# Layer 1's modulation: one product with ones against transposes and a sum along the free axis

## The chip, the core and the metric

The kernel runs on one core of a Trainium2 chip. The metric is the device time of one execution in microseconds (us). Instructions run on five engines: TensorE (PE in the profile), VectorE (DVE), ScalarE (ACT), GpSimd (POOL) and SyncE (SP, which issues the weight transfers). Engines are tied together by semaphores that the kernel sets and waits for by hand.

## The reference, cut to what matters

Two blocks follow each other, each of two layers. The first block is a transformer with a modulation: a vector c (and c_ctx for the context tokens) is passed through silu, multiplied by a 1024 x 6144 matrix of the layer, and the six slices of the result shift, scale and gate the layer's activations.

```
for i in range(DEPTH):                       # DEPTH = 2
    mod_lat = (silu(c) @ w_mod[i] + b_mod[i])
    mod_ctx = (silu(c_ctx) @ w_mod[i] + b_mod[i])
    sh1, sc1, gt1, sh2, sc2, gt2 = split(mod_lat, 6)
    ...
    x_lat = x_lat + gt1 * mix
    x_lat = x_lat + gt2 * sq_relu_mlp(modulate(rms_norm(x_lat, g2), sh2, sc2), w_mlp1[i], w_mlp2[i])
```

What the change touches is silu(c) @ w_mod[1] and silu(c_ctx) @ w_mod[1] alone: 2 x 6144 numbers, which layer 1 needs.

## The kernel before, in words

Layer 1's modulation is computed while layer 0's MLP runs, long before it is needed. The MLP of layer 0 has 16 weight slots of 1024 x 512, in the order up, up, down, down, four times over (`mlp_slots`). Slot j is worked off in four granules m = 0 to 3. A granule is one product of 24 matmuls: the weights are split into a rounded part hi and a rest lo, and eight chunks k are each multiplied three times (L1160 to L1162, `split_product`), for 512 tokens, into one bank of PSUM. ACT makes hi (L1586), DVE makes lo (L2008) into one of two pairs of buffers, so ACT can start the hi of the granule after the next only when a product has been filled in. For an up granule ACT then makes the squared relu (L1717 to L1720) and DVE its rest (L2166); for a down granule DVE adds the result to x (L2089).

Behind each slot j below 12 (`N_LATE`) the weight ring brings a slot of w_mod[1]. DVE's `late_partial(j, q)`, called at granule q of slot j, behind the work on that granule's product, adds two of the eight chunks, scaled by silu(c) and silu(c_ctx), into an accumulator of 128 partitions x 512 columns for each of the two vectors s (L1970, L1974). After q = 3 the accumulators `mod_acc[:, j % 2]` of slot j are complete (semaphore `acc_ready`) but still have to be added over the 128 partitions. TensorE does that: `late_sum(j - 1)`, behind all four granules of slot j, multiplies each 128 x 128 piece by a column of ones (L1134), eight products of one column each. All 12 sums write different columns of one bank, number 3, under the single key "modsum"; so TensorE waits for that bank to be free only once, and DVE reads it only once, at slot 12 (`mod_biased(1, 0, 48, ("modsum",))`). DVE waits in `await_acc_free` before it overwrites an accumulator two slots later.

Every bank has two counters: `filled`, raised by TensorE with the last matmul of a key (`fill`), and `drained`, raised by the reader (`drain`). `start_bank(key)` makes TensorE wait until all earlier users of the bank are drained. The order on each engine is the order of the code, nothing reorders it.

Of the kernel before, what the change touches and what calls it, by code (L numbers as in the profile page):

```python
# [11 lines left out]
ALU = mybir.AluOpType  # L12
ACT = mybir.ActivationFunctionType
AX_X = mybir.AxisListType.X

P = 128
# [39 lines left out]
N_LATE = 12  # L56
# [132 lines left out]
def plan_banks():  # L189

    use, count = {}, [0] * 8

    def take(key, bank):
        use[key] = (bank, count[bank])
        count[bank] += 1

    for t in range(4):
        for g in range(2):
            take(("x", t, g), 2 * t + g)
    take(("prm", 0), 0)  # L200

    def unit_plan(tag, units):
        ms = rot = 0
        for name, kind, banks in units:
            for n, b in enumerate(banks):
                take((tag, name, n), b)
            if kind == "norm":
                take((tag, name, "ms"), 4 + ms % 2)
                ms += 1
                if is_roped(name):  # L210
                    take((tag, name, "rot"), 6 + rot % 2)
                    rot += 1

    for i in range(DEPTH):
        tag = ("a", i)
        take((tag, "n1"), 4)
        if i == 0:
            for n in range(MOD_FIRST):
                take((tag, "modrow", n), 5 + n % 3)
            take((tag, "modA"), 6)  # L220
            for s in range(1, 2 * DEPTH):
                take(("prm", s), s)
        unit_plan(tag, units_a(i))
        unit_plan(tag, units_m(i))
        if i == 0:
            for n in range(MOD_FIRST, MOD_FIRST + MOD_ATTN):
                take((tag, "modrow", n), 7)
            take((tag, "modB"), 7)
        for u in range(4 * len(groups_of(i))):
            take((tag, "s", u), u % 4)  # L230
            take((tag, "t", u), 4 + u % 2)
        for g in range(len(groups_of(i))):
            take((tag, "o", g), 6)
        for c in range(2):
            take((tag, "pool", c), 7)
        for m in range(KC):
            take((tag, "wout", m), m % 4)
        take((tag, "n2"), 4)
        for m in range(FF // P):
            take((tag, "up", m), m % 3)  # L240
        if i == 0:
            take((tag, "modsum"), 3)
        for n in range(BLOCKS):
            for m in range(KC):
                take((tag, "down", n, m), 4 + m % 4)
    for l in range(DEPTH):
        tag = ("b", l)
        take((tag, "lam"), 5)
        take((tag, "n1"), 4)
        unit_plan(tag, units_b())  # L250
        for n in range(4):
            take((tag, "av", n), n)
        for n in range(4):
            take((tag, "bv", n), n)
        take((tag, "bif"), 4)
        for u in range(UNITS):
            take((tag, "s", u), 0)
            take((tag, "w", u), 1)
            take((tag, "t", u), 2)
        take((tag, "gT"), 4)  # L260
        for p in range(2 * NH2):
            take((tag, "o", p), 3)
            take((tag, "oT", p), 4)
        for j, (name, c) in enumerate(MID):
            take((tag, name, c), 5 + j % 3)
        for name in AFTER:
            for c in range(8):
                take((tag, name, c), c % 4)
    for t in range(2):
        for g in range(2):  # L270
            take(("out", t, g), 2 * t + g)
    return use
# [115 lines left out]
def program(nc, A, out):  # L388
# [10 lines left out]
    with ExitStack() as ctx:  # L399
# [13 lines left out]
        def sem(name):  # L413
            return ctx.enter_context(nc.semaphore(name))
# [36 lines left out]
        def cc(name, rows=P, n=None):  # L451
            o, w = CONST[name]
            return cst[0:rows, o:o + (n or w)]

        IDENT = cc("ident")
# [101 lines left out]
        silu_tanh = sem("silu_tanh")  # L557
        silu_made = sem("silu_made")
        acc_ready = sem("acc_ready")
        acc_used = sem("acc_used")  # L560
        late_used = sem("late_used")
        modA_made = sem("modA_made")
        modB_made = sem("modB_made")
# [39 lines left out]
        def bank(key):  # L603
            return ps[:, use[key][0], :]

        def await_bank(eng, key):
            b, n = use[key]
            eng.wait_ge(filled[b], n + 1)
# [9 lines left out]
        def drain(ins, key):  # L618
            ins.then_inc(drained[use[key][0]], 1)
# [7 lines left out]

        def await_acc_free(eng, j):

            eng.wait_ge(acc_used, j + 1)  # L630

        def gain(s, row, rows=P):
            return prm[0:rows, s, row:row + 1]
# [374 lines left out]
        def _(pe):  # L1008
# [4 lines left out]
            def start_bank(key):  # L1013
                b, n = use[key]
                assert seen[b] == n, (key, b, n, seen[b])
                seen[b] += 1
                if n:

                    pe.wait_ge(drained[b], n)
                return ps[:, b, :]  # L1020

            def fill(ins, key):
                ins.then_inc(filled[use[key][0]], 1)
# [99 lines left out]
                        last = mm(b[:, 2 * j:2 * j + 2], mod_row(n)[:, m * P:(m + 1) * P], four[:, 0:2], start=True, stop=True)  # L1123
                fill(last, key)

            def late_sum(j):

                key = (("a", 0), "modsum")
                b = start_bank(key) if j == 0 else bank(key)
                pe.wait_ge(acc_ready, 2 * (j + 1))  # L1130
                for m in range(4):
                    for s in range(2):
                        col = 2 * (4 * j + m) + s
                        last = mm(b[:, col:col + 1], mod_acc[:, j % 2, s, m * P:(m + 1) * P], cc("ones", P, 1),  # L1134
                                  start=True, stop=True)
                if j == N_LATE - 1:
                    fill(last, key)
                else:
                    last.then_inc(acc_used, 1)


            source = [None]
# [48 lines left out]
            for i in range(DEPTH):  # L1191
# [157 lines left out]
                for j, (name, _, _) in enumerate(mlp_slots(i)):  # L1349
                    for m in range(4):  # L1350
                        n = first_gran["mlp", i] + 4 * j + m
                        if (j, m) == (0, 0):
                            split_products_in_step(n, lambda k: h_hi[:, k, t0:TOK], lambda k: h_lo[:, k, t0:TOK], TOK - t0)
                        elif (j, m) == (0, 1):
                            continue
                        elif name == "up":
                            split_product(n, lambda k: h_hi[:, k, t0:TOK], lambda k: h_lo[:, k, t0:TOK], TOK - t0)
                        else:
                            if (4 * j + m) % 16 == 8:

                                source[0] = (up_ready, n // 16 * KC, 1)
                            split_product(n, lambda k: hid_hi[:, k, t0:TOK], lambda k: hid_lo[:, k, t0:TOK], TOK - t0)
                    if i == 0 and 1 <= j <= N_LATE:
                        late_sum(j - 1)


            pe.wait_ge(consts_made, 2)
# [498 lines left out]
        def _(dve):  # L1866
# [93 lines left out]
            def late_partial(j, q):  # L1960
# [19 lines left out]
                if q == 3:  # L1980

                    dve.wait_ge(acc_ready, 2 * (j + 1))
                    dve.nop().then_inc(late_used, 2)

            def newton(key, parts, T, width):

                n = n_r[0]
                dve.wait_ge(rstd_ready, n + 1)
                n_r[0] += 1
                r, r2 = rstd[0:parts, n % 2, 0:T], nt[0:parts, n % 2, 0:T]  # L1990
                drain(V.scalar_tensor_tensor(r2, bank(key)[0:parts, 0:T], width * EPS, r2, ALU.add, ALU.mult), key)  # L1991
                await_drained(dve, key)
                link(V.scalar_tensor_tensor(r, r2, 3.0 * width, r, ALU.subtract, ALU.mult))
                return n
# [99 lines left out]
            for i in range(DEPTH):  # L2094
# [63 lines left out]
                for g in range(g0, g1):  # L2158
                    key = granules[g][2]
                    lo_to(split_by(key))  # L2160
                    if key[1] == "up":
                        n = n_hid[0]
                        n_hid[0] += 1
                        k = key[2] % KC
                        dve.wait_ge(hid_ready, n + 1)
                        V.tensor_tensor(hid_lo[:, k, t0:TOK], sq[:, n % SQ, 0:TOK - t0],  # L2166
                                        hid_hi[:, k, t0:TOK].bitcast(F32), ALU.subtract).then_inc(up_ready, 1)
                    else:
                        residual(key, key[3], i, 40, s0)
                        if i == DEPTH - 1 and key[2] == BLOCKS - 1 and key[3] == KC - 2:  # L2170
                            lo_to(first_gran["b", 0] + 1)
                    j, q = divmod(g - g0, 4)
                    if i == 0 and j < N_LATE:
                        late_partial(j, q)
                    if i == 0 and (j, q) == (N_LATE, 3):

                        mod_biased(1, 0, 48, ("modsum",))
                        mod_scaled(1, 8, RA["g1"], 0, modA_made)
                        mod_scaled(1, 32, RA["g2"], 1, modB_made)

# [204 lines left out]
```

## Time and profile before

| | |
|---|---|
| median of 3 runs | 1853.84 us (1850.66 to 1855.83) |
| profiled execution, its own time | 1854.16 us |
| its span in the profile | 1852.4 us |
| mean granted TensorE clock | 0.978 of full speed |
| PE, DVE, ACT, POOL busy | 95%, 60%, 47%, 25% of the span |
| chain that ended last, by engine | PE 90%, DVE 4%, ACT 2% |

The time of an execution is the span plus 1.8 us that lie around it. The stage in question, from the first `late_partial` to the last `late_sum`, lies between about 365 and 656 us of the span. In a row of the timeline the first number is the start, the second the duration. The duration of a PE row reaches past the start of the next one, because matmuls are pipelined; so what a matmul costs is read from the distance of two starts, not from its duration.

### The profile page before, as it was taken

What the parts mean: (1) busy time and instruction counts of PE and PEld (TensorE: products, weight loads), DVE (VectorE), ACT (ScalarE), POOL (GpSimd) and SP (SyncE); (2) the same over time, 40 slices, a digit from 0 to 9 for tenths busy, and PEclk for the clock granted to TensorE, in tenths of its full rate; (3) what the DMA queues carried; (4) which work ended last, traced back from release to release, by engine and by line L of the source; (5) the groups of instructions that cost most, each with busy time, mean ns of one, the idle gap of its engine ahead of it and who ended that gap; (6) DMA issues with size and microseconds to landing.
All of it is one profiled execution on the core that took longest, in us unless ns stands there. A gap on an engine that the chain in (4) does not pass through costs nothing.

```text
span 1852.4 us, 28647 instructions
## 1 busy us (share of the span) xinstructions
PE 1766.9 (95%) x10804; PEld 1441.0 (78%) x10804; DVE 1107.5 (60%) x1971; ACT 877.0 (47%) x1741; POOL 460.8 (25%) x864
## 2 busy tenths in 40 slices
PE   4999999899999998989899989999999899999998
PEld 2453464588888886746899989899899898898998
DVE  3327841687777633285555568577555685785555
ACT  2327631332323243274555556566554475674542
POOL 2014201000000002150000016128772152287730
PEclk8899989899999999999999999999999999999999
DMA  8321631254445431210444443543335344432351
GB/s 313 110 88 46 228 137 46 88 184 175 175 173 173 175 100 58 91 46 1 160 180 179 179 167 106 186 151 120 137 137 182 137 149 171 148 138 101 130 197 54
DMA packets 139876, 255.27 MB, mean 138 GB/s; under 512 B 14926, under 2 KB 21724, under 8 KB 139612
## 3 DMA queue, kind: packets, MB, share of 16 engines
q1 hardware_dynamic: 138742, 251.16, 38.4%
q8 instruction: 88, 1.44, 0.3%
q0 software_dynamic: 704, 2.10, 0.3%
q14 instruction: 48, 0.39, 0.1%
q10 hardware_dynamic: 294, 0.18, 0.0%
HBM read 252.38 MB, written 1.05 MB: 137 GB/s over the span
## 4 chain that ended last, share of the span: by engine, by line
PE 90%; DVE 4%; ACT 2%; SPq 1%; issue 1%; DMA 1%; ACTq 0%; POOL 0%; DVEq 0%; POOLq 0%
PE ps L1160 18%; PE ps L1162 18%; PE ps L1161 18%; PE ps L1185 10%; PE ps L1298 2%; PE ps L1040 2%; PE ps L1399 2%; PE ps L1397 2%; PE ps L1398 2%; PE ps L1324 2%; PE ps L1310 1%; PE ps L1067 1%; PE ps L1134 1%; SPq L820 1%; PE ps L1477 1%
## 5 line engine op out<-in xcount | busy, mean ns | idle before, releaser
L1586 ACT ACTIVATE big_r<-ring 128x1024 fp32r<-128x1024 f32 x198 | 209.4, 1060 | 390.1 <-PE ps L1162 376.6
L2008 DVE TENSOR_TENSOR big_r<-ring,big_r 128x1024 fp32r<-128x1024 f32 x198 | 245.2, 1240 | 229.3 <-ACT big_r L1586 228.6
L1161 PE MATMUL ps<-big_r 128*128 128x256 f32 (+1 forms) x1088 | 360.5, 331 | 0.0
L1160 PE MATMUL ps<-hT_r,big_r 128*128 128x256 f32 (+1 forms) x848 | 270.0, 318 | 0.0
L1162 PE MATMUL ps<-hT_r,big_r 128*128 128x256 f32 (+1 forms) x848 | 265.4, 313 | 0.0
L907 POOL TENSOR_TENSOR sq<-sq 128x256 f32<-128x256 f32 (+1 forms) x30 | 36.6, 1220 | 772.0 <-ACT sq L1546 772.0
L1161 PEld LDWEIGHTS ps<-big_r 128*128 128x128 f32 x1088 | 206.8, 190 | 19.1
L1185 PE MATMUL ps<-hT,ring 128*128 128x512 f32 (+1 forms) x544 | 192.9, 515 | 10.5 <-ACT hT L1607 8.9
L1160 PE MATMUL ps<-big_r 128*128 128x256 f32 (+1 forms) x592 | 195.8, 331 | 1.4 <-DVE big_r L2166 1.4
L1162 PE MATMUL ps<-big_r 128*128 128x256 f32 (+1 forms) x592 | 194.8, 329 | 0.0
L1185 PEld LDWEIGHTS ps<-hT,ring 128*128 128x128 f32 x544 | 105.7, 196 | 94.9 <-issue 84.5
L1162 PEld LDWEIGHTS ps<-hT_r,big_r 128*128 128x128 f32 x848 | 161.5, 190 | 9.6
L1160 PEld LDWEIGHTS ps<-hT_r,big_r 128*128 128x128 f32 x848 | 161.6, 191 | 9.3
L1160 PEld LDWEIGHTS ps<-big_r 128*128 128x128 f32 x592 | 112.5, 190 | 12.1 <-DVE big_r L2166 2.2
L2008 DVE TENSOR_TENSOR cst_r<-ring,w_ukv_sb_r 128x1024 fp32r<-128x1024 f32 x70 | 87.4, 1248 | 57.0 <-ACT w_ukv_sb_r L1586 56.9
L1162 PEld LDWEIGHTS ps<-big_r 128*128 128x128 f32 x592 | 112.5, 190 | 10.1
L1586 ACT ACTIVATE w_ukv_sb_r<-ring 128x1024 fp32r<-128x1024 f32 x70 | 74.2, 1059 | 95.8 <-PE ps L1162 83.7
L1974 DVE SCALAR_TENSOR_TENSOR pT<-ring,csilu,pT 128x512 f32<-128x512 f32 x168 | 118.5, 747 | 1.3
L1160 PE MATMUL ps<-hT_r,w_ukv_sb_r 128*128 128x256 f32 x384 | 111.9, 291 | 0.0
L1162 PE MATMUL ps<-hT_r,cst_r 128*128 128x256 f32 x384 | 108.2, 282 | 0.0
L1161 PE MATMUL ps<-xT_r,w_ukv_sb_r 128*128 128x256 f32 x384 | 107.7, 281 | 0.0
L1991 DVE SCALAR_TENSOR_TENSOR nt<-ps,nt 128x256 f32<-128x256 f32 (+3 forms) x74 | 38.9, 526 | 109.0 <-ACT nt L1558 108.6
(312 smaller groups left out, 4184.2 us busy)
## 6 DMA issues: line engine op xcount, KB each, us to landing
ring<-in_w_in SPq DMA_DIRECT2D x42, 2048.0 KB, 7.9
ring<-in_w_mlp SPq DMA_DIRECT2D x32, 2048.0 KB, 7.7
ring<-in_w_mod SPq DMA_DIRECT2D x24, 2048.0 KB, 7.9
ring<-in_w_out SPq DMA_DIRECT2D x4, 2048.0 KB, 8.0
ring<-in_w_out_a SPq DMA_DIRECT2D x4, 2048.0 KB, 8.0
ring<-in_w_out_b SPq DMA_DIRECT2D x4, 2048.0 KB, 7.9
ring<-in_w_o SPq DMA_DIRECT2D x4, 2048.0 KB, 8.0
ring<-in_w_in SPq DMA_DIRECT2D x12, 256.0 KB, 5.1
```

The source lines that it names most:

```text
L1040: last = mm(b[0:parts, 0:T], ones, sq[0:parts, n % SQ, 0:T], start=(j == 0), stop=(j == chunks - 1))
L1160: mm(b[:, 0:T], w_hi[:, k, :], hi(k), start=(k == 0), stop=False)
L1161: mm(b[:, 0:T], w_hi[:, k, :], lo(k), start=False, stop=False)
L1162: last = mm(b[:, 0:T], w_lo[:, k, :], hi(k), start=False, stop=(k == KC - 1))
L1185: last = mm(b[0:cols, 0:T], w[:, k, m:m + cols], src(k), start=(k == 0), stop=(k == KC - 1))
L1298: fill(mm(banks[e][:, 0:tiles * P], lhs, rhs, start=True, stop=True), (tag, "s", 2 * j + e))
L1324: last = mm(b[rows, 0:SEQ], v, weights_T(g, e)[:, t, :], start=(t == 0), stop=(t == tiles - 1))
L1397: mm(o, x_hi, y_hi, start=(m == 0 and k == 0), stop=False)
L1586: act_fn(hi, raw, ACT.Copy).then_inc(hi_ready, 1)
L1974: ins = V.scalar_tensor_tensor(acc, w, c, acc, ALU.mult, ALU.add)
L1991: drain(V.scalar_tensor_tensor(r2, bank(key)[0:parts, 0:T], width * EPS, r2, ALU.add, ALU.mult), key)
L2008: V.tensor_tensor(lo, raw, hi.bitcast(F32), ALU.subtract).then_inc(lo_ready, 1)
```

## The change

`late_sum` goes. In its place `late_transposed(j, s)` transposes the four 128 x 128 pieces of one accumulator into bank 3 (four transposes, 512 columns), and DVE's new `late_reduced(j, s)` adds each piece of 128 columns along the free axis, from PSUM straight into `mod`. There are two of each for a slot, one for each vector s, each with a bank key of its own. TensorE runs the two behind granules m = 0 and m = 2 of the next slot, DVE reduces at q = 1 and q = 3 of it, behind `late_partial`. The bias, which was added while the sums were read, is now added in SBUF at the end.

```diff
         if i == 0:
-            take((tag, "modsum"), 3)
+            for j in range(N_LATE):
+                for s in range(2):
+                    take((tag, "late", j, s), 3)
...
         def await_acc_free(eng, j):
-            eng.wait_ge(acc_used, j + 1)
+            await_bank(eng, (("a", 0), "late", j, 1))
...
-            def late_sum(j):
-                key = (("a", 0), "modsum")
-                b = start_bank(key) if j == 0 else bank(key)
+            def late_transposed(j, s):
+                key = (("a", 0), "late", j, s)
+                b = start_bank(key)
                 pe.wait_ge(acc_ready, 2 * (j + 1))
                 for m in range(4):
-                    for s in range(2):
-                        col = 2 * (4 * j + m) + s
-                        last = mm(b[:, col:col + 1], mod_acc[:, j % 2, s, m * P:(m + 1) * P], cc("ones", P, 1),
-                                  start=True, stop=True)
-                if j == N_LATE - 1:
-                    fill(last, key)
-                else:
-                    last.then_inc(acc_used, 1)
+                    last = tr(b[:, m * P:(m + 1) * P], mod_acc[:, j % 2, s, m * P:(m + 1) * P], IDENT)
+                fill(last, key)
...
-                    if i == 0 and 1 <= j <= N_LATE:
-                        late_sum(j - 1)
+                        if i == 0 and 1 <= j <= N_LATE and m % 2 == 0:
+                            late_transposed(j - 1, m // 2)
...
+            def late_reduced(j, s):
+                key = (("a", 0), "late", j, s)
+                await_bank(dve, key)
+                drain(V.tensor_reduce(mod[:, 1, 4 * j:4 * j + 4, s], bank(key)[:, :].rearrange("p (m k) -> p m k", m=4), AX_X,
+                                      ALU.add), key)
...
                     if i == 0 and j < N_LATE:
                         late_partial(j, q)
+                    if i == 0 and 1 <= j <= N_LATE and q % 2:
+                        late_reduced(j - 1, q // 2)
                     if i == 0 and (j, q) == (N_LATE, 3):
-                        mod_biased(1, 0, 48, ("modsum",))
+                        bias = prm[:, 1, RA["b_mod"]:RA["b_mod"] + 48].unsqueeze(2).to_broadcast([P, 48, 2])
+                        await_drained(dve, (tag, "late", N_LATE - 1, 1))
+                        link(V.tensor_tensor(mod[:, 1, :, :], mod[:, 1, :, :], bias, ALU.add))
```

TensorE, before, behind the fourth granule of slot 2 (down). `pT` is the memory of the accumulators, `cst` the constants, here the ones; a product that starts behind it names its waits.

```order
L1161 MATMUL ps<-big_r 128x512
L1162 MATMUL ps<-big_r 128x512
L1134 MATMUL ps<-cst,pT 128x1 [waits acc_ready]
L1134 MATMUL ps<-cst,pT 128x1 x7
L1160 MATMUL ps<-big_r 128x512 [waits lo_ready,bank4_drained]
L1161 MATMUL ps<-big_r 128x512
```

TensorE, after, behind the first granule of slot 2; the two rows of L1133 stand a second time behind its third granule. The lines of the product are now L1155 to L1157, and `cst` is the identity.

```order
L1156 MATMUL ps<-big_r 128x512
L1157 MATMUL ps<-big_r 128x512
L1133 MATMUL ps<-cst,pT 128x128 [waits acc_ready,bank3_drained]
L1133 MATMUL ps<-cst,pT 128x128 x3
L1155 MATMUL ps<-big_r 128x512 [waits lo_ready,bank5_drained]
L1156 MATMUL ps<-big_r 128x512
```

What moved: the adding over partitions comes three granules earlier, is cut in two groups, and each group now waits for the bank's reader as well.

VectorE, before, the last two granules of slot 2. `big_r<-ring,big_r` is the lo of a later granule, `xT<-ps,mod,xT` the work on the product, `pT<-ring,csilu,pT` is `late_partial`.

```order
L2008 TENSOR_TENSOR big_r<-ring,big_r 128x1024 [waits hi_ready]
L2089 SCALAR_TENSOR_TENSOR xT<-ps,mod,xT 128x256 [waits bank7_filled]
L2089 SCALAR_TENSOR_TENSOR xT<-ps,mod,xT 128x256
L1974 SCALAR_TENSOR_TENSOR pT<-ring,csilu,pT 128x512 [waits dve_chain,slot1_landed]
L1974 SCALAR_TENSOR_TENSOR pT<-ring,csilu,pT 128x512 [waits dve_chain] x3
L2008 TENSOR_TENSOR big_r<-ring,big_r 128x1024 [waits acc_ready,hi_ready]
```

VectorE, after, the same place.

```order
L2010 TENSOR_TENSOR big_r<-ring,big_r 128x1024 [waits hi_ready]
L2091 SCALAR_TENSOR_TENSOR xT<-ps,mod,xT 128x256 [waits bank7_filled]
L2091 SCALAR_TENSOR_TENSOR xT<-ps,mod,xT 128x256
L1969 SCALAR_TENSOR_TENSOR pT<-ring,csilu,pT 128x512 [waits dve_chain,slot1_landed]
L1969 SCALAR_TENSOR_TENSOR pT<-ring,csilu,pT 128x512 [waits dve_chain] x3
L1984 TENSOR_REDUCE mod<-ps 128x4 [waits acc_ready,bank3_filled]
L2010 TENSOR_TENSOR big_r<-ring,big_r 128x1024 [waits hi_ready]
```

What moved: one reduction of 512 columns stands behind the four operations of `late_partial`, ahead of the next lo.

## Rows read from the trace of the kernel before

**Rows 1.** The page: busy time of PE; then PE and clock in 40 slices.

```profile
PE 1766.9 (95%) x10804; PEld 1441.0 (78%) x10804; DVE 1107.5 (60%) x1971; ACT 877.0 (47%) x1741; POOL 460.8 (25%) x864
...
PE   4999999899999998989899989999999899999998
...
PEclk8899989899999999999999999999999999999999
```

**Rows 2.** Busy by stretch: length, PE, PEld, DVE, ACT, POOL, clock, DMA share, GB/s.

```profile
365.00:656.00 291.00, 291.00 (x1381) 244.07 (x1379) 221.10 (x317) 98.47 (x129) 0.00 (x0) 1.00 0.51 181
...
800.00:860.00 60.00, 53.88 (x274) 26.91 (x274) 50.55 (x109) 43.43 (x97) 23.47 (x31) 1.00 0.00 1
```

**Rows 3.** Waits between 360 and 660: waiter, released by; total, times, longest.

```profile
ACT big_r L1586 <- PE ps L1162: 190.5, 49, 6.2
DVE big_r L2008 <- ACT big_r L1586: 58.0, 44, 3.4
```

**Rows 4.** Line L1134's instructions, min/median/max ns; then its pieces of the chain.

```profile
L1134 PE MATMUL ps<-cst,pT x192: 164/250/250, 394.6 to 655.9; 128*128 128x1 f32 x192
...
394.77 1.68 PE ps L1134 x16
418.38 1.68 PE ps L1134 x16
...
654.45 1.68 PE ps L1134 x16
```

**Rows 5.** Timeline of PE around the late sum of slot 0: start, duration.

```profile
394.38 0.39 PE L1162 MATMUL ps<-hT_r,big_r 128*128 128x512 f32 x1
394.61 1.84 PE L1134 MATMUL ps<-cst,pT 128*128 128x1 f32 x16
396.31 0.49 PE L1160 MATMUL ps<-big_r 128*128 128x512 f32 x1
396.64 0.40 PE L1161 MATMUL ps<-big_r 128*128 128x512 f32 x1
```

**Rows 6.** Timeline in attention: transposes back to back, and after a wait for DVE.

```profile
841.63 0.60 PE L1310 MATMUL ps<-cst,sq 128*128 128x128 f32 x4
842.07 1.88 PE L1298 MATMUL ps<-big 96*128 96x512 f32 x4
...
191.51 0.63 PE L1310 MATMUL ps<-cst,pb 128*128 128x128 f32 x4 [0.54 <-DVE pb L2126]
192.07 1.08 PE L1324 MATMUL ps<-pT,big 128*64 128x256 f32 x8
...
856.71 0.48 DVE L2126 TENSOR_SCALAR pb<-pb,stat 128x512 f32<-128x512 f32 x1
...
857.34 0.63 PE L1310 MATMUL ps<-cst,pb 128*128 128x128 f32 x4 [0.59 <-DVE pb L2126]
```

**Rows 7.** Timeline of ACT and DVE behind an up granule (slot 1, m = 3).

```profile
394.89 1.06 ACT L1586 ACTIVATE big_r<-ring 128x1024 fp32r<-128x1024 f32 x1 [2.56 <-PE ps L1162]
...
395.98 1.23 DVE L2008 TENSOR_TENSOR big_r<-ring,big_r 128x1024 fp32r<-128x1024 f32 x1
397.80 0.69 DVE L2166 TENSOR_TENSOR big_r<-sq,big_r 128x512 fp32r<-128x512 f32 x1 [0.59 <-ACT big_r L1720]
398.41 2.86 DVE L1974 SCALAR_TENSOR_TENSOR pT<-ring,csilu,pT 128x512 f32<-128x512 f32 x4
```

**Rows 8.** The same behind a down granule (slot 2, m = 3).

```profile
418.50 1.06 ACT L1586 ACTIVATE big_r<-ring 128x1024 fp32r<-128x1024 f32 x1 [4.38 <-PE ps L1162]
...
421.51 2.86 DVE L1974 SCALAR_TENSOR_TENSOR pT<-ring,csilu,pT 128x512 f32<-128x512 f32 x4
```

**Rows 9.** Line L2116: DVE's reductions of scores from PSUM, ns.

```profile
L2116 DVE TENSOR_REDUCE stat<-ps x72: 406/681/693, 180.5 to 855.9; 128x1 f32<-128x512 f32 x48, 128x1 f32<-128x256 f32 x24
```

**Rows 10.** Timeline: end of late_partial(0, 3), and ACT behind granule (1, 0).

```profile
376.93 2.86 DVE L1974 SCALAR_TENSOR_TENSOR pT<-ring,csilu,pT 128x512 f32<-128x512 f32 x4
...
378.57 1.06 ACT L1586 ACTIVATE big_r<-ring 128x1024 fp32r<-128x1024 f32 x1 [2.28 <-PE ps L1162]
```

More of the change, by code:

```diff
@@ L559, in program @@
         acc_ready = sem("acc_ready")
-        acc_used = sem("acc_used")
         late_used = sem("late_used")
@@ L1354, in _ @@
                         elif (j, m) == (0, 1):
-                            continue
+                            pass
                         elif name == "up":
```

## The prediction, made before the changed kernel ran

> **What bounds the kernel now.** I read the page first: PE is busy 95% of the span and 9 tenths or more in nearly every slice [rows 1]. Then the stage that the change touches: from 365 to 656 us PE is busy for all of the 291 us at a granted clock of 1.00, which is the 2.4 GHz level, while DVE has 221.10 us of work, 76% [rows 2]. The waits of that stage tell who follows whom: ACT waits for products, 190.5 us in all, DVE waits for ACT, 58.0 us, and PE waits for nobody [rows 3]. So every microsecond taken from PE here is gained, every one added or waited is lost, and DVE's 24% of idle time costs nothing as long as no product waits for DVE. The chain of waits holds the products with ones as well, 12 pieces at a regular distance [rows 4].
>
> **What is removed.** 96 products with ones, 192 instructions in the trace. One late sum starts at 394.61 and the next product at 396.31, 1.70 us; that product's first step then takes 0.33 us (396.31 to 396.64) where 0.23 us is usual (394.38 to 394.61), so 1.80 us in all [rows 5]. Twelve of them: -21.6 us. This also gives the length of a granule: the late sums of slots 0 and 11 start 259.68 us apart, 11 periods of 23.61 us [rows 4]; less 1.80 that is 21.81, a quarter of it 5.45 us.
>
> **What is added on PE, without waits.** 24 groups of four transposes of 128 x 128 fp32. The trace has the very form in attention: four take 0.44 us when PE comes to them without a pause (841.63 to 842.07), and 0.56 us when it comes to them out of a wait (191.51 to 192.07) [rows 6]. I add 0.10 us for the slower first step of the product behind, as behind the ones. That is 0.54 us for a group not waited for and 0.66 us for one behind a wait. If no group waits: 24 x 0.54 = 13.0 us, and the change gains 8.6 us.
>
> **What is added on DVE.** 24 reductions of 512 columns from PSUM; the nearest rows, the maxima over 512 scores, take 0.68 us, with 0.41 us as the least of the line for 256 columns [rows 9]. I take 0.68 us; the sum of these on DVE, 16 us, lies in its idle time. The last bias operation reads SBUF instead of PSUM and lies ahead of nothing that PE needs for 60 us; I put it at nothing.
>
> **The waits.** Here the cover of before is gone. Before, a late sum of slot j - 1 stood behind all four granules of slot j, some 22 us after the accumulators' last granule, and it never waited for the bank after the first time. Now a group waits for two things on DVE:
> - the first group of slot j's accumulators, one granule behind (j, 3), waits for `late_partial(j, 3)` and for bank 3, which is free once DVE has reduced the last group of slot j - 1. That reduction stands behind `late_partial(j, 3)`.
> - the second group, behind (j + 1, 2), waits for the reduction of the first, which stands behind `late_partial(j + 1, 1)`.
>
> So in both cases PE has done exactly one granule, 5.45 us, since the product that set DVE going. What does DVE need from that product on? In an up slot: PE starts what stands behind the product at 394.61 [rows 5]; ACT makes a hi from 394.89, DVE the lo from 395.98, waits for ACT's squares until 397.80, and `late_partial` runs from 398.41 to 401.27 [rows 7]. That is 6.66 us after 394.61. The reduction follows: 7.34. PE starts 0.15 us after the operation that it waited for has ended (856.71 + 0.48 = 857.19, and 857.34) [rows 6]: 7.49. Less 5.45, PE stands still for 2.04 us. In a down slot ACT starts at 418.50, which puts the start behind the product at 418.22 (0.28 earlier, as above), and `late_partial` ends at 424.37 [rows 8]: 6.15 + 0.68 + 0.15 - 5.45 = 1.53 us.
>
> This time doesn't shrink from group to group: the whole of DVE's row of work is set off by the fill of a product, so a PE that has waited does not find DVE ahead the next time. Nor does the reduction delay anything else for long: in an up slot DVE has 0.59 us of waiting for ACT behind the lo [rows 7], in a down slot its end at 6.83 us lies beside the next lo, which can't start before about 6.8. Queued behind the waiting transposes on PE are only products, and behind the reductions on DVE the next lo, which PE needs a granule later.
>
> How many: slots 1 to 11 contain 5 up (1, 4, 5, 8, 9) and 6 down. Each kind of group waits once for each of them: 10 waits of 2.04 = 20.4 us and 12 of 1.53 = 18.4 us. The very first group waits for the accumulators alone, which are ready at 376.93 + 2.86 = 379.79, while PE would be there at 378.57 - 0.28 = 378.29 [rows 10]: 1.65 us with the 0.15. The last group needs no wait, slot 12 has no `late_partial`. Together 40.4 us. Bounds of this term: nothing, if DVE's row is somehow covered; 33 us, if the reduction ends 0.3 us earlier on average; 47 us, if it costs 0.3 us more, as behind a semaphore wait.
>
> **Sum.** -21.6 + 23 x 0.66 + 0.54 + 40.4 = +34.5 us on the profiled execution's 1854.2, so 1888.7; the median of the runs lies 0.3 us below it: 1888.
>
> The Trainium skill, "Perfetto Trace Analysis", section "Optimizing Tensor Performance", says that independent matmul groups should rotate through different PSUM banks so that emptying one overlaps the next group's matmuls. The change does the opposite, two groups for a slot in one and the same bank. The row above agrees with the rule: of 2.04 us the bank's share over the accumulator's is the reduction's 0.68 us at the first group, and all of it at the second.
>
> **The rivals.**
> 1. *No wait binds, and the change saves what it seems to.* For it: DVE idles 24% of the stage. Against it: that idle time lies in front of the lo, before the work on the product, not behind it. Time: 1853.8 - 8.6 = 1845.
> 2. *Only the accumulator binds, bank 3 doesn't:* only 12 first groups wait, 5 x 1.36 + 6 x 0.85 + 1.65 = 13.6 us (the waits above without the reduction), 12 x 0.66 + 12 x 0.54 = 14.4 us of transposes, less 21.6: +6.4 us, 1860. It would take an emptying of the bank that comes ahead of `late_partial`, which DVE's order does not show.
> 3. *The clock falls.* With the waits PE is busy about 88% of the stage (40 of 325 us idle). If a tenth of it went at 1.2 GHz, 0.1 x 291 = 29 us would come on top: 1917. Against it: from 800 to 860 us PE is busy 53.88 of 60 us in short pieces, and the granted clock is 1.00 [rows 2].
>
> The Trainium skill, "TensorE: Matmul & The Clock Gate", section "A second HAM failure mode: psum-queue depth-cycling", has a kernel in which short idle times between matmul groups that cycle through banks let the clock swing between its two levels; that would be rival 3. The trace here speaks against it, with the 1.00 of that window.
>
> **How the numbers follow.** Forecast as worked out: 73%, from 1879 to 1899. Rival 1: 8%. Rival 2 and anything between it and the forecast: 11%. Rival 3: 8%. The range reaches from 1866, part of the way to rival 2, to 1899. A difference of 0.3%, 5.6 us, is about what a measurement of this kernel can tell from none. Faster: rival 1, 0.07; same: 0.03; slower: 0.90.
>
> **What would show it.** Right: in the waits of the stage, rows of PE's transposes waiting for DVE's reduction (22 times, 1.5 and 2.0 us) and once for the accumulators; granules still 5.45 us; periods of a slot of about 21.8 + 2 x 0.66 + 4.08 = 27.2 us in an up slot and 26.2 in a down slot, where they were 23.61; everything behind the stage merely later by some 34 us. Wrong: no idle time of PE ahead of the transposes; transposes that take much more than 0.11 us each; reductions far from 0.68 us; a granted clock below 1.00 in the stage.

## The result, and the profile after

The changed kernel is slower: 1886.84 us (median of 4 runs, 1885.09 to 1889.61) against 1854.84 us (4 runs), a ratio of 1.0172 with a 95% interval of 1.0156 to 1.0188. The prediction was 1888, from 1866 to 1899.

The page after, its first rows and the two slices that answer to [rows 1]. The digits of PE in slices 9 to 14, which lie in the stage of layer 0's MLP, were 9 and are 8 now; the clock's row has not moved.

```profile
span 1883.3 us, 28502 instructions
...
PE 1762.4 (94%) x10708; PEld 1426.2 (76%) x10708; DVE 1120.3 (59%) x1995; ACT 875.6 (46%) x1741; POOL 460.5 (24%) x864
...
PE   4999999888888899899899989999999899999998
...
PEclk8899989899999999999999999999999999999999
```

The stage by the view of stretches, as in [rows 2] (length, PE, PEld, DVE, ACT, POOL, clock, DMA share, GB/s). Before, PE was busy for all of it; now for 289.28 of 325 us, still at a granted clock of 1.00.

```profile
365.00:690.00 325.00, 289.28 (x1301) 233.64 (x1300) 234.29 (x340) 98.35 (x129) 0.00 (x0) 1.00 0.45 159
```

The waits between 360 and 700 us (waiter, released by; total, times, longest). PE, which waited for nobody [rows 3], waits 22 times for DVE's reduction (L1984) and once for an accumulator (L1969).

```profile
ACT big_r L1581 <- PE ps L1157: 230.1, 52, 7.0
DVE big_r L2010 <- ACT big_r L1581: 82.9, 28, 5.1
...
PE ps L1133 <- DVE mod L1984: 34.2, 22, 2.0
...
PE ps L1133 <- DVE pT L1969: 1.5, 1, 1.5
```

The chain that ended last, in order of time (start, duration), behind an up granule. Before, this stretch of the chain was products alone. Now it leaves PE at the fill, runs through ACT and the whole of `late_partial`, and comes back 7.6 us later.

```profile
396.25 0.24 PE ps L1157
...
396.60 1.06 ACT big_r L1581
397.66 0.49 ACT sq L1712
398.17 0.64 ACT sq L1714
398.84 0.64 ACT big_r L1715
399.54 0.57 issue
400.11 0.76 DVE pT L1969
400.89 2.09 DVE pT L1969 x3
403.12 0.70 DVE mod L1984
403.87 0.66 PE ps L1133 x4
```

The same behind a down granule. The way back to PE takes 6.9 us here, 0.7 less: 0.5 because ACT makes no squares, and 0.2 because this is the reduction at q = 1. The one above is at q = 3, where DVE first waits for the end of `late_partial` (`acc_ready`).

```profile
409.76 0.24 PE ps L1157
...
410.11 1.07 ACT big_r L1581
411.24 1.10 issue
412.35 0.87 DVE xT L2091 x2
413.21 0.67 DVE pT L1969
413.91 2.08 DVE pT L1969 x3
415.99 0.61 DVE mod L1984
416.64 0.66 PE ps L1133 x4
```

One group in PE's timeline. From the start of the last matmul of the product to the transposes it is 2.09 us where 0.23 is usual, so 1.86 us are lost; the view says 1.71 because it counts from the matmul's modelled end, 0.15 later. I add 0.15 us to each shown wait below.

```profile
388.24 0.39 PE L1157 MATMUL ps<-hT_r,big_r 128*128 128x512 f32 x1
390.33 0.66 PE L1133 MATMUL ps<-cst,pT 128*128 128x128 f32 x4 [1.71 <-DVE mod L1984]
390.75 0.47 PE L1155 MATMUL ps<-hT_r,big_r 128*128 128x512 f32 x1
391.06 0.39 PE L1156 MATMUL ps<-big_r 128*128 128x512 f32 x1
```

How much of it is the stage's? Its length is best taken from the first operation of `late_partial` to the first sum of squares of layer 1, which stands behind the whole MLP. The rows are of before (L1970, L1052), then of after (L1965, L1053).

```profile
L1970 DVE TENSOR_SCALAR pT<-ring,csilu x24: 476/480/485, 365.1 to 618.1; 128x512 f32<-128x512 f32 x24
...
723.73 1.10 PE L1052 MATMUL ps<-sq,cst 128*128 128x512 f32 x2 [2.16 <-POOL sq L907]
```

```profile
L1965 DVE TENSOR_SCALAR pT<-ring,csilu x24: 475/479/485, 362.2 to 642.2; 128x512 f32<-128x512 f32 x24
...
750.80 2.05 PE L1053 MATMUL ps<-sq,cst 128*128 128x512 f32 x2 [2.16 <-POOL sq L908]
```

358.6 us before, 388.6 us after: 30.0 us, where the spans differ by 30.9 and the medians by 32.0. Below, "the stage" with a length is always this stretch.

### The profile page after: what moved, and what is told of

It is laid out like the page before. It is cut to its first block, busy times and chain, and to the rows that moved or that the text cites. A ratio compares the mean times of both kernels' runs of the same rounds, so it can differ in the third digit from the quotient of the medians.

```text
span 1883.3 us, 28502 instructions
## 1 busy us (share of the span) xinstructions
PE 1762.4 (94%) x10708; PEld 1426.2 (76%) x10708; DVE 1120.3 (59%) x1995; ACT 875.6 (46%) x1741; POOL 460.5 (24%) x864
## 4 chain that ended last, share of the span: by engine, by line
PE 81%; DVE 9%; ACT 4%; issue 2%; SPq 1%; DMA 1%; ACTq 0%; POOL 0%; DVEq 0%; POOLq 0%
PE ps L1155 15%; PE ps L1157 15%; PE ps L1156 15%; PE ps L1180 10%; DVE pT L1969 4%; PE ps L1293 2%; ACT big_r L1581 2%; PE ps L1041 2%; PE ps L1394 2%; PE ps L1392 2%; PE ps L1393 2%; PE ps L1319 2%; PE ps L1305 1%; PE ps L1068 1%; SPq L821 1%
## 5 line engine op out<-in xcount | busy, mean ns | idle before, releaser
L1156 PE MATMUL ps<-big_r 128*128 128x256 f32 (+1 forms) x1088 | 360.4, 331 | 0.0
L1155 PE MATMUL ps<-hT_r,big_r 128*128 128x256 f32 (+1 forms) x848 | 270.5, 319 | 0.0
L1157 PE MATMUL ps<-hT_r,big_r 128*128 128x256 f32 (+1 forms) x848 | 265.5, 313 | 0.0
L1156 PEld LDWEIGHTS ps<-big_r 128*128 128x128 f32 x1088 | 206.9, 190 | 18.7
L1155 PE MATMUL ps<-big_r 128*128 128x256 f32 (+1 forms) x592 | 196.3, 332 | 1.4 <-DVE big_r L2168 1.4
L1157 PE MATMUL ps<-big_r 128*128 128x256 f32 (+1 forms) x592 | 194.8, 329 | 0.0
L1157 PEld LDWEIGHTS ps<-hT_r,big_r 128*128 128x128 f32 x848 | 161.5, 190 | 9.5
L1155 PEld LDWEIGHTS ps<-hT_r,big_r 128*128 128x128 f32 x848 | 161.6, 191 | 9.1
L1155 PEld LDWEIGHTS ps<-big_r 128*128 128x128 f32 x592 | 112.5, 190 | 11.7 <-DVE big_r L2168 2.2
L1157 PEld LDWEIGHTS ps<-big_r 128*128 128x128 f32 x592 | 112.5, 190 | 10.2
L1969 DVE SCALAR_TENSOR_TENSOR pT<-ring,csilu,pT 128x512 f32<-128x512 f32 x168 | 118.5, 747 | 1.3
L1155 PE MATMUL ps<-hT_r,w_ukv_sb_r 128*128 128x256 f32 x384 | 111.8, 291 | 0.0
L1157 PE MATMUL ps<-hT_r,cst_r 128*128 128x256 f32 x384 | 108.2, 282 | 0.0
L1156 PE MATMUL ps<-xT_r,w_ukv_sb_r 128*128 128x256 f32 x384 | 107.7, 281 | 0.0
```

Of the source, the lines that this page charges most:

```text
L1155: mm(b[:, 0:T], w_hi[:, k, :], hi(k), start=(k == 0), stop=False)
L1156: mm(b[:, 0:T], w_hi[:, k, :], lo(k), start=False, stop=False)
L1157: last = mm(b[:, 0:T], w_lo[:, k, :], hi(k), start=False, stop=(k == KC - 1))
L1969: ins = V.scalar_tensor_tensor(acc, w, c, acc, ALU.mult, ALU.add)
```

## The experiments

The theory: PE loses its time in waits for DVE, because a group of transposes stands one granule behind the fill that sets DVE's row of work going, and the reduction ends that row. The rival: the 24 reductions are simply too much for DVE in this stage, wherever they stand. Each run below was compared with the kernel before on the same chip (1854.6 to 1855.4 us).

**e1: the reduction first.**

```diff
-                    if i == 0 and j < N_LATE:
-                        late_partial(j, q)
                     if i == 0 and 1 <= j <= N_LATE and q % 2:
                         late_reduced(j - 1, q // 2)
+                    if i == 0 and j < N_LATE:
+                        late_partial(j, q)
```

> The changed kernel with DVE's reduction put ahead of late_partial of the same granule instead of behind it; nothing else moves. Theory (PE waits for DVE's row of work, one granule after the fill): the second groups find bank 3 drained about 4.4 us after the fill, before PE needs it at 5.45, so their 11 waits (5 of about 1.9, 6 of 1.4 us) and 11 restarts of 0.12 us go, 19 us in all. The first groups still wait, since late_partial(j, 3) now ends 0.6 us later. 1887 - 19 = 1868 us. Rival (the 16 us of reductions overload DVE in the stage, so products get their weights late): same work, 1887 us.

Measured: 1864.82 us, ratio 1.0050 (1.0031 to 1.0069). The waits of the stage, in the same view:

```profile
PE ps L1133 <- DVE pT L1969: 18.3, 12, 1.8
```

The 22 waits for the bank are gone; 12 are left, all for the accumulators. The work on DVE is the same, so the rival falls. The run is 22 us faster than the changed kernel, where 19 were expected. The stage is 20.0 us shorter (368.6 us), and PE's timeline gives the same: 19.2 us less waiting and 0.9 us less for the transposes. The other 2 us are less than the runs of this kernel alone differ by (4 us).

**e2: the second group in another bank.** The order of every engine stays as in the changed kernel.

```diff
-                for s in range(2):
-                    take((tag, "late", j, s), 3)
+                if i == 0 and 1 <= j <= N_LATE and m == 0:
+                    take((tag, "late", j - 1, 0), 3)
+                if i == 0 and 1 <= j <= N_LATE and m == 2:
+                    take((tag, "late", j - 1, 1), 7 if name == "up" else 0)
...
+                        await_drained(dve, (tag, "late", N_LATE - 1, 0))
                         await_drained(dve, (tag, "late", N_LATE - 1, 1))
+                        await_drained(dve, (tag, "late", N_LATE - 2, 1))
```

The two added waits stand ahead of the bias. The edit also lists the banks of all up and down products slot by slot; each keeps the bank that it had.

> The changed kernel with the second group of a slot in another bank: bank 7 in up slots, bank 0 in down slots, where no product of the slot uses it; order on all engines unchanged. Theory: the second groups wait for nothing (19 us less), the first groups only for the accumulators, 0.7 us less each, 11 x 0.7 = 8 us: 1887 - 27 = 1860 us, the figure of the prediction's rival 2. Rival (DVE overloaded by the reductions): 1887 us.

Measured: 1869.29 us, ratio 1.0077 (1.0061 to 1.0093), 9 us more than expected. The waits between 360 and 700 us show why: beside the 11 waits for the accumulators there is one of 6.9 us, of a product (L1156) for a reduction.

```profile
PE ps L1134 <- DVE pT L1970: 11.0, 11, 1.5
...
PE ps L1156 <- DVE mod L1985: 6.9, 1, 6.9
```

It was a flaw of the experiment. The first product of slot 12 uses bank 0, where the second group of slot 11 lay. DVE reduces that group behind its work on the last product of slot 11, and PE had nothing else to work off after that product. The stretches around it show a second loss: PE went on at half the clock. The clock had fallen inside the pause, 2 us after its start, and PE's next 13 matmuls took 5.65 us, 2.7 us more than at full clock.

```profile
630.00:638.00 8.00, 8.00 (x38) 6.38 (x36) 7.87 (x12) 1.06 (x1) 0.00 (x0) 1.00 0.71 262
638.00:645.00 7.00, 0.12 (x2) 0.03 (x1) 5.62 (x9) 1.06 (x1) 0.00 (x0) 0.66 0.00 0
645.00:647.00 2.00, 2.00 (x5) 1.61 (x6) 0.00 (x0) 0.00 (x0) 0.00 (x0) 0.50 0.71 231
...
651.00:653.00 2.00, 2.00 (x11) 1.61 (x10) 0.00 (x0) 0.00 (x0) 0.00 (x0) 1.00 0.04 14
```

**e7: the same with the bank mended.** In down slots the second group takes, of banks 0 to 2, the one that the next up slot needs last.

```diff
-                    take((tag, "late", j - 1, 1), 7 if name == "up" else 0)
+                    take((tag, "late", j - 1, 1), 7 if name == "up" else (1, 0, 2)[j // 4])
```

> As the kernel with two banks, but with the second group's bank in down slots chosen by what the next up slot needs last (1, 0, 2 in turn) in place of always bank 0, which the first product of slot 12 needs at once: there PE stood still for 6.9 us and then ran 12 matmuls at half the clock. Theory: that 6.9 us and some 2.5 us of slow clock go, nothing else changes; waits of the first groups for the accumulators remain, 12.7 us by that run's trace, with 11 us of transposes less 21.6: 2 us above before, 1857 us, where the run with the flaw had 1869. Rival (part of the loss is DVE's load of reductions, whatever the bank): 1865 us or more.

Measured: 1857.68 us (10 runs), ratio 1.0017 (1.0008 to 1.0027), as expected. Of the waits these remain:

```profile
PE ps L1134 <- DVE pT L1970: 11.7, 12, 1.5
```

A second bank alone takes 29 of the 32 us away by the medians, and 26.6 of the 30.0 us of the stage (362.0 us long here). What is left waits for the accumulators, one granule behind `late_partial(j, 3)`.

**e3: both moved, one bank.** Groups behind granules 1 and 3, reductions two granules later or at the next slot's first, ahead of `late_partial`.

```diff
-                        if i == 0 and 1 <= j <= N_LATE and m % 2 == 0:
+                        if i == 0 and 1 <= j <= N_LATE and m % 2:
...
-                    if i == 0 and j < N_LATE:
-                        late_partial(j, q)
-                    if i == 0 and 1 <= j <= N_LATE and q % 2:
-                        late_reduced(j - 1, q // 2)
+                    if i == 0 and q == 0 and 2 <= j <= N_LATE + 1:
+                        late_reduced(j - 2, 1)
+                    if i == 0 and q == 2 and 1 <= j <= N_LATE:
+                        late_reduced(j - 1, 0)
+                    if i == 0 and j < N_LATE:
+                        late_partial(j, q)
-                    if i == 0 and (j, q) == (N_LATE, 3):
+                    if i == 0 and (j, q) == (N_LATE + 1, 0):
```

The last pair of lines moves the bias behind the last reduction.

> The changed kernel with the groups behind granules m = 1 and m = 3, two granules apart from late_partial(j, 3), and the reductions at q = 2 and at q = 0 of the next slot, ahead of late_partial. Bank 3 alone is used. Theory: no group waits; what is left is 24 x 0.54 us of transposes for the 21.6 us of products with ones: 8.6 us below the kernel before, 1846 us. Rival (DVE overloaded): above 1870 us. If transposes cost more among the products than 0.54 us a group, it is this run that shows it.

Measured: 1844.70 us (6 runs, 1841.06 to 1845.60), ratio 0.9942 (0.9929 to 0.9956). It beats the changed kernel by 42 us and the kernel before by 10 (by the stage 10.7, 348.0 against 358.7 us). No wait of PE is left in the stage; the row answers to [rows 2]:

```profile
365.00:656.00 291.00, 291.00 (x1330) 240.88 (x1330) 238.75 (x344) 103.38 (x136) 0.00 (x0) 1.00 0.51 181
```

DVE has more work here than before (238.75 against 221.10 us) and is in nobody's way. The timeline of PE gives the price of a group that isn't waited for: 0.36 us for the four transposes and 0.08 for the slower first step behind, 0.44 together.

```profile
384.33 0.39 PE L1157 MATMUL ps<-hT_r,big_r 128*128 128x512 f32 x1
384.56 0.60 PE L1133 MATMUL ps<-cst,pT 128*128 128x128 f32 x4
384.92 0.48 PE L1155 MATMUL ps<-hT_r,big_r 128*128 128x512 f32 x1
385.23 0.40 PE L1156 MATMUL ps<-big_r 128*128 128x512 f32 x1
```

**e5: the groups moved, the reductions not ahead.** As e3, but with the two `late_reduced` behind `late_partial`.

> As the kernel with both moved, but with the reductions behind late_partial of their granule (q = 2, and q = 0 of the next slot); the groups stay behind m = 1 and m = 3. Theory: PE waits again at nearly every group, since it comes one granule after the fill that sets the reduction's row going: 2.0 or 1.5 us where the reduction is at q = 2, 0.5 us less where it is at q = 0 (late_partial is shorter there): about 5 x 2.0 + 6 x 1.4 + 4 x 1.4 + 6 x 0.9 = 29 us, with 15.7 us of transposes less 21.6: 23 us above before, 1877 us. If it were the accumulators alone for which PE waited, moving the groups away from late_partial(j, 3) would be enough: 1846 us.

Measured: 1872.77 us, ratio 1.0094 (1.0072 to 1.0117); 4 us less than expected: by PE's timeline the transposes cost 4 us less and the waits 2 us less than in the sum, and the kernel before took 1 us more in this comparison.

```profile
PE ps L1133 <- DVE mod L1984: 23.4, 21, 1.7
```

Not one wait for an accumulator is left, and 21 for the reduction. So moving the groups without the reductions mends only one of the two waits.

**e6: a short reduction.**

```diff
-                bank(key)[:, :].rearrange("p (m k) -> p m k", m=4), AX_X,
+                bank(key)[:, :].rearrange("p (m k) -> p m k", m=4)[:, :, 0:8], AX_X,
```

> The changed kernel with the reduction over the first 8 instead of all 128 columns of each piece (32 instead of 512 elements a partition); the sums of layer 1's modulation are incomplete. Theory: every one of the 22 waits for bank 3 ends about 0.5 us earlier, 11 us: 1876 us. If the waits were only the accumulators' (the reduction beside them): 1887 us.

Measured: 1875.44 us, ratio 1.0115 (1.0097 to 1.0132): 11 us less than the changed kernel, as expected. The line of the reduction (min/median/max ns) after and here, and the waits here:

```profile
L1984 DVE TENSOR_REDUCE mod<-ps x24: 681/685/693, 389.6 to 687.0; 128x4 f32<-128x512 f32 x24
```

```profile
L1984 DVE TENSOR_REDUCE mod<-ps x24: 184/188/193, 391.8 to 678.2; 128x4 f32<-128x32 f32 x24
...
PE ps L1133 <- DVE mod L1984: 23.3, 22, 1.5
```

0.50 us less for each reduction, and 34.2 - 23.3 = 10.9 us less waiting, 0.50 for each of 22. So a wait of PE for the bank ends with DVE's reduction.

**e8 and e9: the reduction done twice, four times.**

```diff
-                drain(V.tensor_reduce(...), key)
+                for again in range(2):            # e9: range(4)
+                    ins = V.tensor_reduce(...)
+                    if again < 1:                 # e9: 3
+                        link(ins)
+                drain(ins, key)
```

> The changed kernel with each of the 24 reductions done twice, one after the other. Theory: each of the 22 waits of PE gets longer by a whole reduction with its semaphore, 0.75 us: 16 us more, 1903 us, at an unchanged clock. The pauses are then up to 2.9 us. Rival 3 of the prediction (the clock falls with such pauses): clearly more, with a granted clock below 1.00 between 365 and 690 us.

Measured: 1905.0 us, ratio 1.0282 (1.0256 to 1.0308), 2 us more than expected, but not at an unchanged clock. The waits grew by 16.1 us, 0.73 for each of 22 (34.2 to 50.3 in the view):

```profile
PE ps L1133 <- DVE mod L1985: 50.3, 22, 2.7
```

The stage grew by 20.7 us against the changed kernel. The other 4.6 are the clock's: behind three of the 22 pauses, each of 2.6 us, it was 1.2 GHz for 3.4 us.

> The changed kernel with each reduction done four times. The same sum: 22 x 3 x 0.75 = 50 us more, 1937 us, if the clock holds at pauses of up to 4.4 us; if pauses of this length bring the half clock behind each of the 22, as one of 6.9 us did (about 2.5 us lost), 1990 us.

Measured: 1966.89 us (2 runs), ratio 1.0609 (1.0585 to 1.0634), between the two figures. The waits between 360 and 770 us:

```profile
PE ps L1133 <- DVE mod L1985: 83.2, 23, 4.1
```

The stretch from 365 to 700 us, of e8 and of e9:

```profile
365.00:700.00 335.00, 283.23 (x1253) 228.12 (x1252) 245.91 (x359) 94.31 (x123) 0.00 (x0) 0.98 0.43 151
```

```profile
365.00:700.00 335.00, 262.05 (x1049) 209.33 (x1048) 237.39 (x346) 80.39 (x106) 0.00 (x0) 0.90 0.37 129
```

With pauses of 2.1 to 2.8 us behind the reductions the mean clock was 0.98, with pauses of 3.5 to 4.3 us 0.90; in e9, 20 of the 22 pauses of that length were followed by a stretch at half the clock. The stage of e9 is 81.6 us longer than the changed kernel's: 49.1 us of more waiting, and 32.5 us of slow clock. So rival 3 of the prediction exists, but further out than this change reaches: with its own pauses of 1.4 to 2.1 us the clock did not fall once.

**e4: fewer products with ones.** The kernel before with 1 product instead of 8 behind 11 of the 12 slots.

```diff
-                for m in range(4):
-                    for s in range(2):
+                for m in range(4 if j == N_LATE - 1 else 1):
+                    for s in range(2 if j == N_LATE - 1 else 1):
```

> The kernel before with one product with ones (2 instructions) instead of eight (16) behind each of the slots 1 to 11; the eight of slot 12 stay. So most sums of layer 1's modulation are left out. Theory: 11 x 14 instructions of 0.107 us fewer, 16.4 us: 1854.5 - 16.4 = 1838 us. If products with ones had lain beside other work, 1854 us.

Measured: 1837.43 us, ratio 0.9906 (0.9891 to 0.9922): 17.2 us less. Its timeline has 0.14 us for a late sum of one product, where the eight took 1.70: 11 x 1.56 = 17.2 us. The products with ones lay on the path in full, as the prediction had it.

## Why the prediction was right

- *PE bounds the stage, so all that it does or waits counts.* Right: the stage grew by 30.0 us, and its own terms give 39.2 + 11.9 - 21.6 = 29.5 (below).
- *Removed, 21.6 us.* Right: e4 removes seven of the eight products in 11 of the 12 sums and gains 17.2 us, all that they took in the timeline.
- *The waits, 40.4 us.* Right in number and size: 23 waits, 22 behind the reduction and the first one behind the accumulator. Shown are 34.2 + 1.5 us; with 0.15 for each 39.2. Behind the 10 up granules it was 1.86 us where the reduction stands at q = 1 and 2.10 at q = 3 (predicted 2.04 for both), behind the 12 down granules 1.36 and 1.60 (predicted 1.53). Two small things were wrong in it, and DVE's rows show them. The reduction does not start just where `late_partial` ends: at q = 1 it starts 0.08 us before that end, at q = 3, where DVE waits for `acc_ready`, 0.14 us behind it. And PE starts 0.06 us behind the end of the reduction, not 0.15. With these, 6.66 - 0.08 + 0.68 + 0.06 - 5.45 = 1.87 us at q = 1 and 2.10 at q = 3. In the sum they nearly cancel, so it is only 1.2 us off. The periods of a slot were 26.8 us (up) and 25.8 (down), predicted 27.2 and 26.2.
- *The transposes, 15.7 us.* Mis-sized, by 3.8 us the most of all terms. I took 0.66 us for a group behind a wait and 0.54 for one without, from the transposes in attention [rows 6]. Between products of rounded weights it was 0.50 us (390.33 to 390.75, and 0.08 for the step behind) and 0.44: 23 x 0.50 + 0.44 = 11.9 us. These 3.8 us and the 1.2 of the waits are why the sum of 34.5 lay above the 30.0 us of the stage. The cheaper transposes also explain why e3 gained 10 us and not 8.6, and why e5 came out below.
- *Why the wait doesn't shrink.* Right: all 22 waits came, the last ones as long as the first. In e1, e3 and e7 another order or another bank took them away, while the 24% of idle time that DVE had did not help. Rival 1 (1845 us) was not the result of this change but of e3, once nothing waited.
- *Rival 2, only the accumulator binds (1860 us).* This is what e7 built: 1857.7 us.
- *The rule on rotating banks* in the Trainium skill, "Perfetto Trace Analysis", section "Optimizing Tensor Performance": measured here it is worth 29 us (changed kernel against e7; 26.6 in the stage). But a single bank is enough where the order gives its reader time: e3 keeps bank 3 and is 13 us faster than e7.
- *The clock.* Held at 1.00 in the stage of the changed kernel, through 23 pauses of up to 2.1 us. That is as the prediction had it, though e8 shows that 0.7 us more in each pause already costs some of it.
- *The total, 1888 against 1886.8 us.* That it is so close is in part luck: the sum was 4.5 us too high for the stage, and 2.0 of the 32.0 us between the medians are not the stage's and stood in none of its terms.

Where those 2.0 us lie: in the two profiles the stage begins 2.9 us earlier after than before, and what follows it takes 3.8 us longer (1132.5 against 1128.7 us, at a granted clock of 0.98 against 0.99); with the 30.0 that is the 30.9 between the spans. The last 1.1 us lie between the profiled executions and the medians, which is within what the runs of one kernel differ by. Why the clock behind the stage was lower stays open; the change does not touch that part.

## What to carry to other kernels

When a product is replaced by one that hands its result to another engine, ask not only what the new instructions cost, but what stands between the event that sets the other engine going and the instruction that needs it back. If that distance is one granule and the other engine's row of work is longer than one granule, its mean idle time doesn't help: the wait comes every time. Put the short piece that frees the resource ahead of the long piece that nobody waits for, and the consumer two granules behind its producer; of the orders tried here, only the one with both (e3) turned the change into a saving.

## What the runs showed of the hardware

- Four transposes of 128 x 128 fp32 took 0.36 us between products of rounded fp32 weights (e3) and 0.44 us in attention, where the next product is plain fp32 [rows 6]. What makes the difference no run separates.
- PE's granted clock stayed at 2.4 GHz through 23 pauses of up to 2.1 us with about 11 us of work between them. With pauses of up to 2.8 us the mean was 0.98 (e8), with pauses of 3.5 to 4.3 us 0.90 (e9). A single pause of 7 us went with 10 us at 1.2 GHz, of which PE worked 5.7 and lost 2.7 (e2). The Trainium skill, "TensorE: Matmul & The Clock Gate", section "A second HAM failure mode: psum-queue depth-cycling", has such a swing for short idle times between groups: it was not seen at this change's pauses, seen three times in e8 and at nearly every pause in e9.
- Eight fp32 products of a single column with a 128 x 128 stationary side cost 1.8 us, more than eight transposes of the same data (0.88 us in two groups). The trace has two instructions for such a product, each with a weight load of its own, and one for a transpose; an instruction took 0.11 us in the first case and 0.09 in the second. What sets these times no run separates.
- PE started 0.06 us behind the end of DVE's reduction, which frees the bank (changed kernel, 403.12 + 0.69 and 403.87), but 0.15 us behind the end of a DVE operation that wrote its operand (374.87 + 2.08 and 377.10, as in [rows 6]).
